# Value pages moved to another issuing engine, a reordered group of matmuls and later waits in a hybrid decoder step

## What is computed

```python
def layer(x, ...):
    h = rmsnorm(x, norm1_w)
    z = h @ w_in                      # one projection, split among three head groups
    # A: retention, 4 heads, chunks of 128 positions
    #    o = (q k^T * decay) v   +   (q * gq) S_before_the_chunk
    # B: latent attention, 8 heads: causal over the prompt, and for each decode
    #    sequence over 16 pages of 128 past positions, found by page_table
    #    scores = q_lat . pool_lat[page] + q_rope . pool_rope[page];  o = softmax(scores) . pool_lat[page]
    # C: gated linear recurrence
    x = x + concat(A, B, C) @ w_out
    x = x + conv_ffn(rmsnorm(x, norm2_w))
```

## Time and profile before

| | |
|---|---|
| median of 3 runs | 1709.8 us (1707.3 to 1714.24) |
| the profiled execution: own time, span | 1712.13 us, 1710.5 us |
| busy, share of the span | PE 84%, PEld 74%, DVE 53%, ACT 32%, POOL 1% |
| matmuls of `product` (L1315), six groups | 446.4 + 443.3 + 442.7 + 141.9 + 141.6 + 141.2 us |
| transfers from SP's queue | 133.54 MB, 24.7% of 16 DMA engines |
| transfers from POOL's queue | 11.97 MB, 1.9% |

### The profile page before, as it was taken

How to read it: one execution, slowest core, us unless ns; L and a number is a source line. 1 busy time by engine, 2 the same in 40 slices (tenths; PEclk the granted TensorE clock), 3 DMA queues, 4 the chain that set the end, 5 groups by cost and what they waited for, 6 DMA issues and landing times.

```text
span 1710.5 us, 31164 instructions
## 1 busy us (share of the span) xinstructions
PE 1438.8 (84%) x10850; PEld 1269.8 (74%) x10850; DVE 901.9 (53%) x1540; ACT 546.3 (32%) x854; POOL 24.6 (1%) x49
## 2 busy tenths in 40 slices
PE   4987866457999999999999876654699999999993
PEld 4985422225999999999999743322398999999993
DVE  5586343324476653666656834423436666346664
ACT  3341132213344422333423313311224443223341
POOL 1000000000000000000010000000000000000001
PEclk9997687678999999999999977877799999999997
DMA  7311222221222223222352022222122322232221
GB/s 273 113 56 31 61 79 79 78 79 50 88 80 86 84 84 107 86 98 72 104 185 86 23 73 64 77 78 76 37 101 73 98 87 76 95 111 86 70 93 50
DMA packets 119421, 146.66 MB, mean 86 GB/s; under 512 B 16609, under 2 KB 90626, under 8 KB 119202
## 3 DMA queue, kind: packets, MB, share of 16 engines
q1 hardware_dynamic: 116114, 133.54, 24.7%
q0 software_dynamic: 3216, 11.97, 1.9%
HBM read 141.20 MB, written 4.45 MB: 85 GB/s over the span
## 4 chain that ended last, share of the span: by engine, by line
PE 59%; SPq 13%; issue 6%; DVE 5%; ACT 2%; DMA 1%; DVEq 0%; ACTq 0%; POOL 0%
PE PS L1315 53%; SPq L349 4%; SPq L354 4%; SPq L351 4%; SPq L342 2%; PE PS L1617 1%; DVE RS L838 1%; PE PS L1459 1%; PE PS L1582 1%; DVE STAT L1140 0%; PE PS L1568 0%; PE PS L1330 0%; DMA out_y<-XF 0%; DVE R L915 0%; DVE XNL L832 0%
## 5 line engine op out<-in xcount | busy, mean ns | idle before, releaser
L1315 PE MATMUL PS<-XNH,WH 128*128 128x260 f32 x2176 | 446.4, 287 | 45.2 <-DVE WL L812 30.2
L1315 PE MATMUL PS<-XNH,WL 128*128 128x260 f32 x2176 | 443.3, 286 | 0.0
L1315 PE MATMUL PS<-XNL,WH 128*128 128x260 f32 x2176 | 442.7, 285 | 0.0
L1315 PEld LDWEIGHTS PS<-XNH,WH 128*128 128x128 f32 x2176 | 340.0, 190 | 49.4 <-issue 37.2
L478 ACT ACTIVATE WH<-RAW 128x1024 fp32r<-128x1024 f32 x200 | 211.5, 1057 | 439.3 <-PE PS L1315 361.4
L1315 PEld LDWEIGHTS PS<-XNH,WL 128*128 128x128 f32 x2176 | 339.2, 190 | 0.3
L1315 PEld LDWEIGHTS PS<-XNL,WH 128*128 128x128 f32 x2176 | 338.5, 190 | 0.3
L812 DVE TENSOR_TENSOR WL<-RAW,WH 128x1024 fp32r<-128x1024 f32 x200 | 244.4, 1222 | 169.2 <-ACT WH L478 164.0
L1315 PE MATMUL PS<-HL,WH 128*128 128x260 f32 x704 | 141.9, 283 | 0.0
L1315 PE MATMUL PS<-HH,WL 128*128 128x260 f32 x704 | 141.6, 282 | 0.0
L1315 PE MATMUL PS<-HH,WH 128*128 128x260 f32 x704 | 141.2, 282 | 0.0
(11 more groups left out here) (243 smaller groups left out, 1479.2 us busy)
## 6 DMA issues: line engine op xcount, KB each, us to landing
RAW<-in_units SPq DMA_DIRECT2D x134, 512.0 KB, 3.3
KT<-in_kat SPq DMA_DIRECT2D x256, 64.0 KB, 1.8
VA<-in_ka SPq DMA_DIRECT2D x256, 64.0 KB, 1.8
RAW<-in_units SPq DMA_DIRECT2D x32, 384.0 KB, 3.1
RAW<-in_units SPq DMA_DIRECT2D x32, 320.0 KB, 2.8
RT<-in_kar SPq DMA_DIRECT2D x256, 16.0 KB, 1.7
C<-in_const POOLq DMA_DIRECT2D x1, 2196.0 KB, 10.0
X<-in_x SPq DMA_DIRECT2D x8, 260.0 KB, 3.7
```

The source lines that it names most:

```text
L1315: last = mm(PS[i % 4][0:rows, hb, 0:HB], w, x(kk)[:, hb * HB:(hb + 1) * HB], start=(kk == 0 and s == 0), stop=(kk == total - 1 and s == 2))
```

## The change

Three things are changed; what is computed stays the same.

1. `chunk_in[k]`: each slab of `X` has a semaphore of its own, and `NW` is started first. ACT waits for slab k where it first reads it, POOL for all eight ahead of `C`. DVE's wait for `C` moves from the first weight unit to the first use of the tables, ahead of `rope`.
2. The value pages leave SP's program. POOL loads their page numbers and starts them, between its saves of results for steps 0 to 3 and in a loop for steps 4 to 15. SP's loop holds keys alone.
3. In `ro`, the four products of a chunk with the scores come first and the four with the state after them.

```diff
-        plain = lambda e: e.wait_ge(x_in, 16 * (KD + 1))
+        chunk_in = [sem(f"chunk_in{k}") for k in range(KD)]
+        plain = lambda e: e.wait_ge(x_in, 16)
@@ sync
+            sp.dma_start(NW[:, :], nwd).then_inc(x_in, 16)
             for k in range(KD):
-                sp.dma_start(X[:, k, :], xd[k]).then_inc(x_in, 16)
-            sp.dma_start(NW[:, :], nwd).then_inc(x_in, 16)
+                sp.dma_start(X[:, k, :], xd[k]).then_inc(chunk_in[k], 16)
...
-                    if g < 8:
-                        four_pages(l, (g // 2 % 2) * (GB_ * PAIR), ("keys", "values")[g // 4], g // 2 % 2, g % 2)
-                for k in range(2):
-                    keys_free(l, k)
-                    keys(l, k + 2, k)
-                with sp.Fori(0, (NSTEP - 4) // 2) as it:
-                    for j in range(2):
-                        keys_free(l, it * 2 + (j + 2))
-                        keys(l, it * 2 + (j + 4), j)
-                        values_free(l, it * 2 + j)
-                        values(l, it * 2 + (j + 2), j)
-                for k in range(NSTEP - 2, NSTEP):
-                    values_free(l, k - 2)
-                    values(l, k, k % 2)
+                    if g < 4:
+                        four_keys(l, (g // 2) * (GB_ * PAIR), g // 2, g % 2)
+                with sp.Fori(0, (NSTEP - 2) // 2) as it:
+                    for j in range(2):
+                        keys_free(l, it * 2 + j)
+                        keys(l, it * 2 + (j + 2), j)
@@ gpsimd
-            pool.wait_ge(x_in, 16 * (KD + 1))
+            for k in range(KD):
+                pool.wait_ge(chunk_in[k], 16)
             pool.dma_start(C[:, :], constd).then_inc(tables_in, 16)
             pool.sem_inc(layers_saved, CREDIT)
+            pool.wait_ge(pt_clamped, 1)
...
+                        pool.dma_start(VA[:, s, bb, j * P:(j + 1) * P],
+                                       kav[bass.ds(row, 1), :, :].rearrange("a p n -> p (a n)")).then_inc(values_in[s], 16)
...
                 pool.dma_start(sl(lat_o), Z[:, Z_CKV, :]).then_inc(saved, 16)
+                values(l, 0, 0)
                 wait(pool, "kr_roped", l, 1)
                 pool.dma_start(sl(rope_o), Z[0:32, Z_KR, :]).then_inc(saved, 16)
+                values(l, 1, 1)
...
                 pool.dma_start(sl(pret_o), SS[:, 3, :]).then_inc(saved, 16)
+                values_free(l, 0)
+                values(l, 2, 0)
                 wait_emptied(pool, l, "du")
                 settle(pool)
                 pool.dma_start(sret_o[...], SD[:, :, :]).then_inc(saved, 16)
+                values_free(l, 1)
+                values(l, 3, 1)
+                with pool.Fori(0, (NSTEP - 4) // 2) as it:
+                    for j in range(2):
+                        values_free(l, it * 2 + (j + 2))
+                        values(l, it * 2 + (j + 4), j)
@@ scalar
-            act.wait_ge(x_in, 16 * (KD + 1))
+            act.wait_ge(x_in, 16)
             for k in range(KD - 1):
-                chunk(None, 0, k, next_weight(None, k), lambda: None)
+                chunk(None, 0, k, next_weight(None, k), lambda: act.wait_ge(chunk_in[k], 16))
+            act.wait_ge(chunk_in[KD - 1], 16)
@@ vector
-            dve.wait_ge(x_in, 16 * (KD + 1))
+            dve.wait_ge(x_in, 16)
...
-                dve.wait_ge(tables_in, 16)
                 lo(l, 0)
...
+                dve.wait_ge(tables_in, 16)
                 rope(l, "pkr", Z[0:32, Z_KR, :], ...)
@@ tensor
                 for n in range(4):
                     for h in range(RH):
-                        last = mm(out, VT[...], SM[:, n, o:o + P], start=True, stop=(n == 0))
-                        if n:
-                            last = mm(out, SS[...], QD[...], start=False, stop=True)
+                        last = mm(ro(n, h), VT[...], SM[:, n, o:o + P], start=True, stop=(n == 0))
+                    for h in range(RH * (n > 0)):
+                        last = mm(ro(n, h), SS[...], QD[...], start=False, stop=True)
```

More of the change, by code:

```diff
@@ L338, in one, with four_keys @@
                 sp.dma_start(RAW[:, u % NRAW, 0:width], src).then_inc(raw_full[u % NRAW], 16)
-            def four_pages(l, at, what, s, half):
+            def four_keys(l, at, s, half):
                 _, numbers = nc.values_load_multi_w_load_instructions(
@@ L347, in four_pages @@
                     bb, j = (4 * half + i) // PAIR, (4 * half + i) % PAIR
[L348 to L355, removed]
+                    sp.dma_start(KT[:, s, bb, j * P:(j + 1) * P],
+                                 katd[bass.ds(row, 1), :, :].rearrange("a p n -> p (a n)")).then_inc(keys_in[s], 16)
+                    sp.dma_start(RT[32 * bb:32 * bb + 32, s, j * P:(j + 1) * P],
+                                 karp[bass.ds(row, 1), :, :].rearrange("a p n -> p (a n)")).then_inc(keys_in[s], 16)
             def keys(l, k, s):
                 for half in range(2):
[L359 to L363, removed]
+                    four_keys(l, k * (GB_ * PAIR), s, half)
             def keys_free(l, k):
                 sp.wait_ge(keys_used, l * NSTEP + k + 1)
-                settle(sp)
-            def values_free(l, k):
-                sp.wait_ge(values_used, l * NSTEP + k + 1)
                 settle(sp)
@@ L414, in _, with values, values_free @@
         def _(pool):
-            pool.wait_ge(x_in, 16 * (KD + 1))
+            for k in range(KD):
+                pool.wait_ge(chunk_in[k], 16)
             pool.dma_start(C[:, :], constd).then_inc(tables_in, 16)
             pool.sem_inc(layers_saved, CREDIT)
+            pool.wait_ge(pt_clamped, 1)
+            def values(l, k, s):
+                for half in range(2):
+                    _, numbers = nc.values_load_multi_w_load_instructions(
+                        PT_SB[0:1, bass.ds(k * (GB_ * PAIR) + 4 * half, 4)], engines=[mybir.EngineType.Pool], min_val=0,
+                        max_val=N_PHYS - 1, skip_runtime_bounds_check_because="Vector has clamped the page numbers to the pool")
+                    for i, page in enumerate(numbers):
+                        row = l * N_PHYS + page
+                        bb, j = (4 * half + i) // PAIR, (4 * half + i) % PAIR
+                        pool.dma_start(VA[:, s, bb, j * P:(j + 1) * P],
+                                       kav[bass.ds(row, 1), :, :].rearrange("a p n -> p (a n)")).then_inc(values_in[s], 16)
+            def values_free(l, k):
+                pool.wait_ge(values_used, l * NSTEP + k + 1)
+                settle(pool)
             with pool.Fori(0, DEPTH) as l:
@@ L1500, in _ @@
                 tile(l, "ro")
+                ro = lambda n, h: ps("ro")[half(h), h // 2, P * n:P * n + P]
                 for n in range(4):
@@ L1503, in _ @@
                         o = 256 * (h % 2) + P * (h // 2)
-                        out = ps("ro")[half(h), h // 2, P * n:P * n + P]
-                        last = mm(out, VT[:, n, HD * h:HD * h + HD], SM[:, n, o:o + P], start=True, stop=(n == 0))
-                        if n:
-                            c = h // 2
-                            last = mm(out, SS[half(h), n - 1, HD * c:HD * c + HD], QD[half(h), c, P * n:P * n + P],
-                                      start=False, stop=True)
+                        last = mm(ro(n, h), VT[:, n, HD * h:HD * h + HD], SM[:, n, o:o + P], start=True, stop=(n == 0))
+                    for h in range(RH * (n > 0)):
+                        c = h // 2
+                        last = mm(ro(n, h), SS[half(h), n - 1, HD * c:HD * c + HD], QD[half(h), c, P * n:P * n + P],
+                                  start=False, stop=True)
                 last.then_inc(full("ro"), 1)
```

## The result

The changed kernel takes 1627.4 us (median of four runs, 1626.1 to 1628.7) against 1712.0 us (1707.3 to 1723.7) for the kernel before in the same comparison: a ratio of 0.950, 95% interval 0.945 to 0.955. The forecast was 1616.6 in a range of 1592 to 1657, and faster. The sum promised 93.2 us, the medians give 84.6. The execution profiled has a span of 1627.2 us, so the two spans differ by 83.3 us.

What follows compares the result with a forecast made beforehand. SP's page starts were taken to bound the decode steps. Value pages 78.8, retention output 9.6 and start 4.8 us sum to 93.2 us, giving 1616.6 us against the median 1709.8, range 1592 to 1657.

Steps and rivals of the forecast that it cites:

- The sum: Whole kernel: 78.8 us from value pages, 9.6 from retention output and 4.8 from the start, 93.2 us saved.
- The reading of the bound: Decode steps 8 to 15: no engine or transfer rate limits; SP's 24 starts a step, 14.65 us, set the pace.
- the rival at 1695 us: Decode steps: transfers bind anyway, only the starts move and the stage stays at 100 us; chance 0.04.
- The value pages: Decode steps in both layers: without value starts on SP, step 15's scores come 38.8 and 40.0 us earlier, 78.8 us.
- Without values a step costs 8.58 us and one of the two leads in turn, in the mean 9.6 us: SP's queue in the decode steps: keys alone take 9.6 us a step, where 14.65 passed before.
- Some 10 us of waiting per layer stay: PE in the decode steps: some 10 us of waits per layer remain, for keys instead of values.
- The rival at 1767 us: Value pages: POOL starts a page only when the former has landed, 19.6 us a step, slower; chance 0.04.
- 26 us a step: Value pages on POOL: estimate from the skill's 3100 ns transfer beside a copy; the kernel would end near 1870.
- The retention output: Tile ro in both layers: ordering products by kind saves 5.8 us in layer 0 and 3.8 in layer 1, 9.6 us.
- A change of kind so costs 0.32 us: Retention output, layer 0: alternating products take 0.62 us against 0.30 in a row; 18 fewer changes save 5.8 us.
- The start: Kernel's beginning: first square at 6.25 us, 4.14 earlier, and DVE loses a 0.64 us wait; gain 4.8 us.
- Behind dc15 nothing waits for pages in either version, and what follows moves along unchanged: After decode step 15, both layers: no page waits and no further gain or loss, 0 us.

Runs made afterwards that it cites:

- the last run: Changed kernel with two added KT/RT buffers for steps 10, 11, 14 and 15, function table loaded ahead of X, GpSimd's twelve value steps written out: 1590.1 us, ratio 0.928.
- staggered order: Changed kernel with each head's state product in the retention output one product later than in the kernel before, kinds still alternating: tile 8.9 us in layer 0, 9.0 in layer 1.
- the start alone: Kernel before with only the waits for each eighth of X and for the constants moved to where they are read: 1710.0 us, ratio 0.998.

## Why the prediction was right, and where it was off

**The reading of the bound held.** SyncE's starts set the pace of the decode steps. Moving a third of them took 73.7 us out of two stretches in which no engine was busy for more than about half the time, and the run with the value pages alone shows it without the other parts. That the transfers themselves bind, the rival at 1695 us, is excluded: the changed kernel gets through the same steps in 65.5 us, at a DMA share of 0.41 in place of 0.28, and the last run, with some keys fetched ahead, in 48.0 us at 0.49. The window in the changed kernel:

```profile
256.04:321.56 65.52, 46.25 (x309) 23.95 (x308) 30.57 (x102) 20.11 (x62) 30.86 (x56) 0.81 0.41 116
```

The Trainium skill (DMA: Bandwidth & Descriptors, "Issuing engines are not separate DMA queues") calls the time to start usually small beside the transfer; here 24 starts a step were the bound, and the measurement decides.

**The value pages were 5 us too high,** in the step "Without values a step costs 8.58 us and one of the two leads in turn, in the mean 9.6 us". It measured 10.29 in layer 0 and 10.2 in layer 1. Over the five steps of layer 0 that is 3.5 us; the sixth, with no lead behind it, gave 1 us back, and the scores of step 15 stood 2.8 us later than forecast. Two single starts lasted five times as long as the others, which the one step of the earlier trace rows could not show. "Some 10 us of waiting per layer stay" was 15.3 and 14.5, now for RT, as named.

**GpSimd kept up,** with the 5.9 us a step worked out from two rows of the start. The rival at 1767 us needed 16 us a step. The Trainium skill (SBUF — State Buffer, "A bandwidth-pool intuition that's wrong (but worth ruling out)") has the 620 and 3100 ns from which 26 us a step were estimated, for a copy on VectorE. For the mix of operations on VectorE here the estimate does not agree with the trace: GpSimd's 256 issues took 0.546 us in the mean, with VectorE busy for 45% of the stretch from 256 to 356 us.

**The retention output was 6.9 us too low,** and two steps share it. "A change of kind so costs 0.32 us" rested on five products in a row at 0.30 us each, but these were the first of the tile. Where the tile begins at a clock of 0.58 to 0.61, the first five, six and eight products took 1.26 us (value pages alone), 1.34 (staggered order) and 1.69 (changed kernel): a further product adds some 0.14 us in the mean, so that about 0.5 us belong to the beginning (an estimate from these three). The staggered order puts a product at 0.075 us and a change at 0.286 at the upper clock, so that nearly all of the old order's time was changes; in layer 1 that is 5.5 us for 3.8. In layer 0 the forecast let the tile stay at the lower clock. There the old order takes 15.66 us at 0.50 and 9.56 at 0.95, so 6.1 of the 11.0 us are the clock's, and 4.9 the order's. The clock's part was not forecast. With the old order the tile ran at the lower clock in both layers of the start alone and mostly at the upper one in both of the value pages alone; these are one execution each, so whether the clock comes with the value pages stays open.

**The start was right** to 0.2 us, with the first square at 6.44 for 6.25. The table load did come to stand behind the wait, and the run that moved it ahead gained those 1.23 us there.

**Not foreseen:** the 5.6 us by which GpSimd's closing drain grew. "Behind dc15 nothing waits for pages in either version, and what follows moves along unchanged" was off by 2.7 us before the output projection, where the granted clock was lower than before, and by this drain at the very end. What sets its length stays open: it is not the number of transfers, not the loop's shape, and reading the address from a table gives no single length.

**The errors partly cancel.** The retention output gave 6.9 us more than forecast, 6.1 of them through a clock that the forecast had not reckoned with. The value pages gave 5.1 us less, and 5.6 were lost at the end, 2.7 ahead of the output projection and 3.6 in all else. That the sum came within 10 us is partly luck; without the retention output's surplus the time would have been some 1634 us, still inside the range.

## What to carry to other kernels

A queue that only starts transfers can be the bound while no engine is busy for more than about half the time and the DMA engines for less than a third. Count its starts per step and multiply by the spacing on its timeline, and when it is relieved, price the next queue in the same way. Where the same queue also stands idle earlier in the stage, added buffers do more than moving starts: 23 us here, against 6 us for the quarter of SyncE's remaining starts that went to GpSimd.

## What the runs showed of the hardware that was not expected

- On TensorE a change between the two kinds of product of the retention output (128 rows and 64 rows) cost 0.286 us at the upper clock (2.4 GHz), about four times a product of 128 columns in a row of its own kind (0.075 us).
- The same 28 products in the same order ran in layer 0 at a granted clock of 0.50 in two kernels (before, and the start alone) and at 0.95 in a third (the value pages alone), 15.66 against 9.56 us in the first and the third. In layer 1 the clock rose within the tile before (0.51 up to 1004.5 us, 1.00 from there, 10.25 us in all) and stayed at 0.51 in the start alone (15.35 us). A part's gain in such a stretch is partly the clock's.
- GpSimd's closing drain lasted 3.75 us without value pages on its queue; with them 9.30 or 9.39 us, but 4.07 and 5.96 us in two of the kernels.
